# Two programs of a hybrid decoder layer re-cut: chunks of 1024 and 2x512 on both, state pass in segments of 512, fewer GpSimd steps in the recurrent path

## What is computed

```python
h = rmsnorm(x, norm_mix)
proj = h @ w_in                       # 1024 -> 512 | 1024 | 1024 | 2048
u_pool, u_rnn, u_gate, g_merge = ...  # g_merge = sigmoid(...), 2 x 1024
y_pool = pool_mixer(u_pool) @ w_pool_out      # trailing means over 2/4/8/16 rows, per-group map
v  = conv4(u_rnn)                             # causal, depthwise
r, i = sigmoid(v @ w_a + b_a), sigmoid(v @ w_x + b_x)   # block-diagonal, 8 heads of 128
a  = sigmoid(lam) ** (8 r);  b = sqrt(1 - a*a) * i * v
hr_t = a_t * hr_{t-1} + b_t                   # along the 4096 rows of a sequence
y_rnn = (hr * gelu(u_gate)) @ w_rnn_out
x = x + (g0 * y_pool + g1 * y_rnn) @ w_o
h = rmsnorm(x, norm_ffn)
x = x + (silu(h @ Wg) * (h @ Wu)) @ w_ffn_out           # 1024 -> 2 x 2816 -> 1024
return rmsnorm(x, norm_final)
```

## Time and profile before

| | us |
|---|---|
| three runs, median (lowest, highest) | 1119.37 (1113.43, 1158.19) |
| the profiled execution, its own time | 1128.91 |
| span of its slowest core (core 6, an even core) | 1127.3 |
| spans of the even cores | 1108.7, 1116.5, 1119.5, 1127.3 |
| spans of the odd cores | 1090.8, 1091.6, 1095.8, 1090.0 |
| core 6: PE, DVE, ACT, POOL busy | 1023.9, 699.2, 518.3, 368.6 |

### The profile page before, as it was taken

One profiled execution on the slowest core, in us unless ns is written; L12 is line 12 of the kernel. 1 busy time (PEld: TensorE's weight loads), 2 busy tenths in 40 slices (PEclk: granted clock), 3 DMA queues, 4 the chain that ended last, 5 costly groups with the idle time before them and its releaser, 6 DMA issues.

```text
span 1127.3 us, 18459 instructions; the slowest of 8 cores (1090.0 to 1127.3 us)
## 1 busy us (share of the span) xinstructions
PE 1023.9 (91%) x4720; PEld 449.7 (40%) x4720; DVE 699.2 (62%) x756; ACT 518.3 (46%) x646; POOL 368.6 (33%) x570
## 2 busy tenths in 40 slices
PE   3989899998899997888999999788999999999994
PEld 2433344433354442333443444333434444444442
DVE  4448975478977448876768878892532533333345
ACT  3276985367666316376366756771411310110112
POOL 3113534245525202434335435453332220120201
PEclk9777788899999998998999999999999999999998
DMA  9533246756427723456477857979599672561613
GB/s 246 81 46 49 56 103 121 141 103 135 92 46 134 151 74 47 66 85 93 96 149 115 126 89 186 210 119 155 88 173 174 130 114 38 84 103 29 103 41 143
DMA packets 58578, 122.16 MB, mean 108 GB/s; under 512 B 6496, under 2 KB 9952, under 8 KB 58464
## 3 DMA queue, kind: packets, MB, share of 16 engines
q0 software_dynamic: 48240, 84.56, 48.4%
q1 hardware_dynamic: 10224, 36.31, 9.4%
HBM read 197.00 MB, written 8.39 MB: 182 GB/s over the span
## 4 chain that ended last, share of the span: by engine, by line
PE 72%; DVE 10%; DMA 6%; ACT 4%; issue 4%; POOL 2%; DVEq 0%; SPq 0%; POOLq 0%; ACTq 0%
PE ps L773 52%; PE ps L1118 12%; PE ps L1063 5%; DVE f_v_f L815 4%; DMA ring_f<-w_in 3%; PE ps L843 2%; PE ps L718 2%; DVE th_f L966 1%; DMA xs<-x 1%; DVE f_v_f L820 1%; DMA X<-x 1%; DVE f_w_f L886 1%; DVE hbt_f L755 1%; DMA ring_f<-w_rnn_out 1%; ACT hbt_f L702 1%
## 5 line engine op out<-in xcount | busy, mean ns | idle before, releaser
L773 PE MATMUL ps<-H_f,ring_f 128*128 128x512 bf16 x2816 | 667.4, 395 | 20.8 <-ACT f_a_f L849 4.9
L773 PEld LDWEIGHTS ps<-H_f,ring_f 128*128 128x128 bf16 x2816 | 277.5, 101 | 389.0 <-issue 140.8
L645 POOL DMA_DIRECT2D ring_f<-w_in x128 | 70.8, 553 | 208.4 <-PE ps L773 151.3
L1093 ACT ACTIVATE th_f<-ps 128x512 f32<-128x512 f32 (+1 forms) x66 | 48.7, 738 | 191.3 <-PE ps L773 183.9
L1118 PE MATMUL ps<-ACW_f 128*128 128x512 bf16 x528 | 119.2, 384 | 0.0
L815 DVE SCALAR_TENSOR_TENSOR f_v_f<-ps,par,f_v_f 128x1023 f32<-128x1023 f32 (+5 forms) x93 | 93.4, 1005 | 30.4 <-PE ps L773 16.6
L645 POOL DMA_DIRECT2D ring_f<-w_ffn_in x88 | 47.4, 539 | 196.9 <-PE ps L773 165.9
L1097 DVE SCALAR_TENSOR_TENSOR th_f<-th_f,ps 128x512 f32<-128x512 f32 (+1 forms) x66 | 56.9, 862 | 73.6 <-ACT th_f L1093 61.8
L1118 PEld LDWEIGHTS ps<-ACW_f 128*128 128x128 bf16 x528 | 52.0, 99 | 63.3 <-issue 4.2
L1003 ACT ACTIVATE th_f<-ps 128x512 f32<-128x512 f32 (+1 forms) x48 | 35.2, 738 | 90.3 <-PE ps L773 87.9
L1124 DVE SCALAR_TENSOR_TENSOR X<-ps,X 128x1024 f32<-128x1024 f32 x36 | 43.7, 1220 | 42.5 <-PE ps L1118 40.3
(11 more groups left out here) (132 smaller groups left out, 1210.1 us busy)
## 6 DMA issues: line engine op xcount, KB each, us to landing
ring_f<-w_in POOLq DMA_DIRECT2D x128, 256.0 KB, 4.8
ring_f<-w_ffn_in POOLq DMA_DIRECT2D x88, 256.0 KB, 4.3
xs<-x SPq DMA_DIRECT2D x24, 512.0 KB, 4.7
ACW_f<-w_ffn_out POOLq DMA_DIRECT2D x44, 256.0 KB, 4.8
X<-x SPq DMA_DIRECT2D x20, 512.0 KB, 5.2
ring_f<-w_rnn_out POOLq DMA_DIRECT2D x24, 256.0 KB, 5.3
ACW_f<-w_o POOLq DMA_DIRECT2D x24, 256.0 KB, 6.0
out<-X SPq DMA_DIRECT2D x12, 512.0 KB, 5.1
```

The source lines that it names most:

```text
L645: it.add(0.55, lambda e: e.dma_start(out=ring[:, w.idx, 0:k, :], in_=src), hold, (w,))
L773: it.add(c_pe(n), lambda e, kc=kc, lo=lo, n=n, b=b: e.matmul(PS[pv.idx // 2][:, pv.idx % 2 + b, 0:n], lhsT=ring[:, w.idx, kc, :], rhs=src[ ...
L1093: it.add(c_act(U), lambda e, U=U, pg=pg, tv=tv: e.activation(out=two(th[:, tv.idx, 0:U], U), in_=P2(pg, U), func=AF.Tanh, scale=0.5), (pg, ...
```

## The change

Both programs get the same cut: c0 of 1024, c1a and c1b of 512. The second program's state pass becomes one segment of 1024, its slots become those of the first (units of 512 rows, 4 base slots, 8 with ACW). In the first program the middle pass is four segments of 512 in two groups; within a group the two segments share the weights of a pair of heads. The extra slots over R and PM become 3, 3, 3, 3, for the first group alone. The copy to hst goes from POOL to DVE in both programs. In the second program some casts, products and last products of the later segments leave POOL (pvt 4 to 2, pbt 1 to 0, pmt 2 to 1); in the first program pat goes from 0 to 2, which puts half of the squares of the middle and later segments on POOL. The w_o blocks are no longer loaded again for c1b. The planner's first pass now counts three ring slots, and two of its cost constants and most tune numbers are new. A path that keeps bf16 weights in HBM (`cache`, `kept`, `win`) is in the code but switched off in both programs (`cache` is False), so `win` is the same as `weight` there.

```diff
@@ tune tables and roles
-    Role(0, (), 1024, ((1024,), (1024,)), (512, 512), 512, 5, (4, 4, 4, 4), (8, 8, 8, 8), (4, 2, 4, 2), True, 3, 4, TUNE0),
-    Role(1024, (512, 512), 768, (), (640, 640), 768, 5, (3, 3, 3, 2), (5, 5, 6, 4), (0, 0, 0, 0), False, 4, 3, TUNE1),
+    Role(0, (), 1024, ((512, 512), (512, 512)), (512, 512), 512, 5, (4, 4, 4, 4), (8, 8, 8, 8), (3, 3, 3, 3), False, 3, 4, False, TUNE0),
+    Role(1024, (1024,), 1024, (), (512, 512), 512, 5, (4, 4, 4, 4), (8, 8, 8, 8), (0, 0, 0, 0), False, 3, 4, False, TUNE1),
...
-         "pbo": 0, "pbt": 3, "pao": 1, "pat": 0}
+         "pbo": 0, "pbt": 3, "pao": 1, "pat": 2}
...
@@ schedule
-        skip = "ring" if order is None else None
+        skip = None
+        if order is None:
+
+            free["ring"] = free["ring"][:-2]
...
-                it.end = dma_free + 2.0
+                it.end = dma_free + 2.6
...
-                    cost += 0.6 * min(cost, max(0.0, heavy - t))
+                    cost += 0.9 * min(cost, max(0.0, heavy - t))
@@ rnn_unit
                 if seg != "c1b":
-                    it = Item("pool", p, tag + ".hs")
-                    it.add(0.25, lambda e: e.tensor_copy(out=hst[:, j:j + 1], in_=F(wv)[:, U - 1:U]),
+                    it = Item("dve", p, tag + ".hs")
+                    it.add(0.16, lambda e: e.tensor_copy(out=hst[:, j:j + 1], in_=F(wv)[:, U - 1:U]),
                            (wv,), (("hst", j),))
@@ merge
-                load_wa(m, wo_d[m], q)
+                if seg != "c1b":
+                    load_wa(m, wo_d[m], q)
```

90 lines of the change are left out of this document (64 added, 26 removed).

## The result

The changed kernel took 1142.09 us (median of 4 runs, 1138.83 to 1145.26); the kernel before, on the same chip, 1120.34. The ratio is 1.0204, with a 95% interval of 1.0164 to 1.0243: slower, clear of noise, though the interval doesn't settle whether by more than 2%. The prediction said 1100, and its range ended at 1132.

What follows compares the result with a forecast made beforehand. The even cores end last, with PE losing time to waits, largest at 420 to 760 us. Terms -13 - 2 - 5 + 1 + 0 = -19 took the median 1119.4 to 1100 us; range 1080 to 1132, own range 1090 to 1110.

Steps and rivals of the forecast that it cites:

- The middle pass in segments of 512: Even cores, 420 to 560 us: shorter bursts of taps spare PE waits; 13 us gained, between 26 gained and 16 lost.
- the second rival: Even cores, 210 to 560 us: middle pass waits for DVE, decided above some 83% busy; 1128 to 1149, middle 1139; chance 0.17.
- no wait above 5 us for the taps: Sign of being right: on an even core the middle pass's matmuls come without a wait above 5 us for L857.
- a middle pass 10 to 15 us shorter: Sign of being right: on an even core the middle pass's stretch up to c1a's start is 10 to 15 us shorter.
- a c0 stage more than 8 us longer: Sign of being wrong: the stage of c0 grows by more than 8 us.
- DVE above 85% busy: Sign of being wrong: DVE above 85% busy over the middle pass, with PE waiting for gates as before.
- Squares on POOL: First program, 24 squares from ACT to POOL slow DVE where both run: 1 us lost, at most 10, at least 0.
- The fourth rival: Contention of the new POOL squares with DVE eats the gain of the bursts: 1116 us; chance 0.10.
- hst off POOL: One-column copies follow the scan at once on DVE, sparing POOL waits: 2 us gained, between 6 gained and 4 lost.
- w_o once: Merges, 760 to 866 us: eight blocks fewer to load, 5 us gained, ends 0 and 9.
- c0's order: First program's c0: gelu, pool and projections reordered, eight copies leave POOL; 0, between 8 gained and 8 lost.
- The odd cores: Second program: 4 us gained, to 1087 to 1092, with 10 to either side; they stay below the even cores.

## Why the prediction was wrong, point by point

**The middle pass in segments of 512: -13 forecast.** This is the step that failed. The DVE work behind it was put at 35 us; the cut alone added 25 (699 to 724), and with the hst copies (6) and the contention of the squares (12) DVE rose by 44. What failed is the sentence that took half of the gain "since the round in the chain is a wait for one long burst and not for a full engine". The gaps in DVE's record there aren't room: they are waits for PE, POOL and ACT in an order that is fixed, and time between steps. At 72% recorded, 461 us took in no more DVE work when 23 to 25 us were added in all, and the even cores became 15 us shorter when 18 were taken. So the second rival had the mechanism, but its rule for when it decides, above 83% busy, came from comparing with 560 to 760 us and was wrong too. That its middle price, 1139, lies so near the 1142 measured is luck in part: 9 of the 24 us are the tail, which it didn't hold.

At 0.6 to 1.2 us per us the 25 us of the cut are worth 15 to 30, and by the accounting below 9 to 12 are left for it. What the shorter rounds give back is thus an estimate of 3 to 21 us, and part of it is visible: the 10 us of less waiting and higher clock between the end of c0's w_o and the end of the mixer's second third. There the longest wait of PE for the taps on core 0 is this one (waited for; us in total, times, longest):

```profile
PE ps L815 <- DVE f_v_f L857: 1.1, 1, 1.1
```

That sign was predicted (no wait above 5 us for the taps) and came true; the longest one of the whole middle pass is 4.2 us on core 0 (4.3 on cores 2 and 6), in the stage before. The sign that stood beside it, a middle pass 10 to 15 us shorter, did not come: the mixer's second third ends 13 us later. One of the signs of being wrong came, a c0 stage more than 8 us longer; the other, DVE above 85% busy, did not. The loss stands from 121 to 339 us, in c0's last units and merge and the first half of the middle units, where the forecast had put no loss. It has two parts: waits (37 us without PE work where 20 were) and the granted clock (0.93 for 0.97, about 7 us of 181).

**Squares on POOL: +1 forecast.** The mechanism was right and the size was off: 5 to 8 us. The bound of one for one held (12 us of DVE for 28 us of squares), but it was applied to the 8 late squares only, because the middle pass was taken to have room. The rule of the Trainium skill named in the prediction (GPSIMD Engine Reference, Specifications and Key points: GpSimd contends with VectorE) pointed the right way, and the trace agrees (scans 57 ns and products 87 ns longer beside the squares). The fourth rival, made from it, reckoned with 16 us and 1116.

**hst off POOL: -2 forecast.** Nothing measurable; both ends of the term hold. DVE takes 0.14 us per copy.

**w_o once: -5 forecast.** 3 us (0 to 6 by the interval). The late merges show it on core 0: from the start of c1a's w_o to the end of c1b's, PE's waits for weights went from 4.2 us to 1.6, and 5.92 MB came in the last 41 us where 6.57 did (144 GB/s for 160).

**c0's order: 0 forecast, 8 either way.** It can't be separated from the segments by these runs: the stages up to the end of c0's w_o lost 28 us on core 0, 3 of them for 16 matmuls more, and the run without small taps gave back 17. The rest stays open between order, clock and contention.

**Not in the sum at all.** The 12 us behind c1b's merge, 9 of them from the planner's new rules. The prediction gave these rules no price. It wrote this stretch off as "the end of the last tile", yet the order there changed too. Moving the norm steps forward returned 1 to 2 us at most; a load of x is next.

**The odd cores: -4 forecast, -14 measured** (1091 to 1077), at the edge of the 10 us given. It has no effect on the time.

**Accounting on the even mean, 24 us:** w_o -2, squares +5 to +8, the rules' part of the tail +9, hst 0; that leaves +9 to +12 for everything else, the segments first of all, and then c0's order. Against the 13 us gained that were forecast this is the largest miss. This split is arithmetic over runs with different edits, not a run of its own. Nor do the runs part DVE's 25 us of the cut from the 30 us that it adds to ACT; extra work on ACT alone wasn't tried. What a table fitted to the new segments without the POOL squares would reach wasn't tried.

## What to carry to other kernels

An engine whose list is in fixed order, and which hands work back and forth with another, can be full well below 100% of recorded busy time. The cheap test is to add a few small steps to it and to take a few away: if the core follows both ways (here 1.1 to 1.2 us for each us added, 0.6 to 0.8 for each taken), every further instruction costs its time, and cutting work into more pieces has to win that back first. Where order comes from a table, undo parts of a change with the order kept; a table under other rules lost 50 us here and says nothing about the part. And a few columns aren't a cheap operation: count small steps at what the trace shows for them, with the gap ahead of each, on whichever engine they are put.

## What the runs showed of the hardware that was not expected

- A multiply and add on one column on POOL has a median of 341 ns and goes up to 4.35 us; 96 of them and 32 on three columns are 77 us. On ACT the one-column step takes 386 to 388 ns, every time.
- After 7.2 us of waits with little PE work between them, 26 matmuls took 8.2 us at a granted clock of 0.5 to 0.6 and then 1, where 5.6 us would do at 0.216 each: the wait was paid one and a third times.
- 24 more POOL products of 1.17 us made 46 DVE scans slower by 57 ns and 46 products by 87 ns on the mean. The scans of 1024 columns in c0, beside which no square was moved, did not change (2334 to 2336 ns).
